# Feed-forward on one core: the first chunk's gate and up products by token tiles, its activations turned by four transposes

## The reference

```python
def swiglu(h, w_gate_up, w_down):
    g, u = jnp.split(h @ w_gate_up, 2, axis=-1)
    return (jax.nn.silu(g) * u) @ w_down
...
h = h + 0.5 * rmsnorm_2(swiglu_2(rmsnorm_2(h, gn[0]), ffn1_w_in[i], ffn1_w_out[i]), gn[1])
```

## Time and profile before

| what | value |
|---|---|
| median of 3 runs | 3369.08 us (3367.74 to 3376.34) |
| span of the profiled execution | 3369.5 us |
| PE busy (matmuls) | 2941.3 us, 87% |
| DVE busy | 1747.3 us, 52% |
| ACT busy | 1295.0 us, 38% |
| POOL busy | 226.9 us, 7% |
| HBM | 153 GB/s over the span |

### The profile page before, as it was taken

One profiled execution on the slowest core, in us unless ns is written; L12 is line 12 of the kernel. 1 busy time (PEld: TensorE's weight loads), 2 busy tenths in 40 slices (PEclk: granted clock), 3 DMA queues, 4 the chain that ended last, 5 costly groups with the idle time before them and its releaser, 6 DMA issues.

```text
span 3369.5 us, 48317 instructions
## 1 busy us (share of the span) xinstructions
PE 2941.3 (87%) x19034; PEld 2651.6 (79%) x19034; DVE 1747.3 (52%) x2004; ACT 1295.0 (38%) x1611; POOL 226.9 (7%) x300
## 2 busy tenths in 40 slices
PE   4977979779799887799899769989889899787799
PEld 4767967579799766699898659989779899775698
DVE  5556455564544544544545345454654544544544
ACT  3334333344333422343444344444443443422443
POOL 1110001110000111100000000000000000112000
PEclk9868988689899878899999779999899999878899
DMA  6445554555655420255454125555445555410353
GB/s 237 166 163 176 186 176 153 175 176 187 206 171 184 138 75 26 97 197 180 166 187 163 57 100 191 184 167 186 147 154 185 166 184 182 129 61 25 124 185 128
DMA packets 348861, 517.09 MB, mean 153 GB/s; under 512 B 9510, under 2 KB 303095, under 8 KB 341559
## 3 DMA queue, kind: packets, MB, share of 16 engines
q1 hardware_dynamic: 342320, 501.81, 44.8%
q0 software_dynamic: 3728, 10.34, 1.0%
q10 hardware_dynamic: 2678, 3.13, 0.3%
HBM read 513.40 MB, written 1.84 MB: 153 GB/s over the span
## 4 chain that ended last, share of the span: by engine, by line
PE 74%; DVE 11%; issue 5%; ACT 4%; DMA 2%; POOL 2%; ACTq 1%; DVEq 0%; POOLq 0%; SPq 0%
PE B L450 15%; PE B L451 15%; PE B L452 15%; PE Y L450 7%; PE Y L452 7%; PE Y L451 7%; DVE w_lo L1338 2%; DVE h_lo L1397 2%; PE Y L807 1%; ACT w_hi L956 1%; ACT junk L967 1%; DVE tmp L1366 1%; DVE x L1369 1%; DVE M L1460 1%; DMA raw<-in_w_ada 1%
## 5 line engine op out<-in xcount | busy, mean ns | idle before, releaser
L1338 DVE TENSOR_TENSOR w_lo<-raw,w_hi 128x2048 fp32r<-128x2048 f32 (+1 forms) x425 | 964.5, 2274 | 690.5 <-ACT w_hi L956 690.2
L450 PE MATMUL B<-h_hi,w_hi 128*128 128x256 f32 x4224 | 1215.3, 288 | 48.1 <-DVE h_lo L1397 19.6
L451 PE MATMUL B<-h_lo,w_hi 128*128 128x256 f32 x4224 | 1207.8, 286 | 0.0
L452 PE MATMUL B<-h_hi,w_lo 128*128 128x256 f32 x4224 | 1206.8, 286 | 0.0
L956 ACT ACTIVATE w_hi<-raw 128x2048 fp32r<-128x2048 f32 (+1 forms) x425 | 804.8, 1900 | 700.9 <-PE B L452 597.7
L450 PEld LDWEIGHTS B<-h_hi,w_hi 128*128 128x128 f32 x4224 | 819.4, 194 | 61.9 <-issue 51.4
L451 PEld LDWEIGHTS B<-h_lo,w_hi 128*128 128x128 f32 x4224 | 816.1, 193 | 5.7 <-issue 2.1
L452 PEld LDWEIGHTS B<-h_hi,w_lo 128*128 128x128 f32 x4224 | 817.1, 193 | 0.0
L450 PE MATMUL Y<-w_hi,a_hi 128*128 128x512 f32 (+1 forms) x810 | 318.1, 393 | 2.6 <-DVE w_lo L1338 2.6
L452 PE MATMUL Y<-w_hi,a_lo 128*128 128x512 f32 (+1 forms) x810 | 317.4, 392 | 0.0
L451 PE MATMUL Y<-w_lo,a_hi 128*128 128x512 f32 (+1 forms) x810 | 316.5, 391 | 0.0
(11 more groups left out here) (222 smaller groups left out, 2938.2 us busy)
## 6 DMA issues: line engine op xcount, KB each, us to landing
raw<-in_ffn_w_in SPq DMA_DIRECT2D x176, 1024.0 KB, 5.0
raw<-in_ffn_w_out SPq DMA_DIRECT2D x88, 1024.0 KB, 4.9
raw<-in_w_ada SPq DMA_DIRECT2D x56, 1024.0 KB, 5.0
raw<-in_w_gate_up SPq DMA_DIRECT2D x44, 1024.0 KB, 5.0
raw<-in_hgrn_w_in SPq DMA_DIRECT2D x32, 1024.0 KB, 5.4
raw<-in_w_down SPq DMA_DIRECT2D x22, 1024.0 KB, 5.0
raw<-in_w_in SPq DMA_DIRECT2D x14, 1024.0 KB, 5.7
raw<-in_diff_w_in SPq DMA_DIRECT2D x12, 1024.0 KB, 5.1
```

Source lines behind the costliest of these rows:

```text
L450: pe.matmul(o, lh, rh, start=first, stop=False)
L451: pe.matmul(o, lh, rl, start=False, stop=False)
L452: return pe.matmul(o, ll, rh, start=False, stop=last)
L1338: dve.tensor_tensor(w_lo[s][:, 0:n], raw[st.r % RING][:, 0:n], w_hi[s][:, 0:n].bitcast(F32), ALU.subtract).then_inc(unit_split, st.step("" ...
```

## The change

The first chunk's gate and up products are done by `first_pair` with `by_tokens`: a 128 by 128 piece of the input is the stationary operand, and 256 columns of the weights move. Each unit then has one half for each tile of tokens, of 8 x 3 = 24 matmuls. I call them gate-0 and gate-1, up-0 and up-1. PE's order is: transposes of tile 0, gate-0, transposes of tile 1, up-0, gate-1, up-1. The results have tokens on the partitions, so the product with silu in `tmp` must be turned for the down product: four transposes into the bank `B[2]`, placed behind the gate product of the second chunk, and `a_hi` and `a_lo` of the first chunk are read from `B[2]`.

```diff
--- before.py
+++ after.py
@@ -575,14 +575,17 @@
                     if t == 0:
                         pe.wait_ge(vector_step, st.at(f"{p}.{('loop', 'last')[i]}.act"))
 
-                whole_input(p)
-                stationary(B[0], f"{p}.first.gate", p)
-                stationary(B[1], f"{p}.first.up")
+                first_pair(p, ((by_tokens(B[0], CH), f"{p}.first.gate"), (by_tokens(B[1], CH), f"{p}.first.up")))
                 st.r += between and 1
                 pe.wait_ge(scalar_step, st.at(f"{p}.first.silu"))
                 stationary(B[0], f"{p}.second.gate")
+                pe.wait_ge(vector_step, st.at(f"{p}.first.mul"))
+                for c in range(2):
+                    for t in range(NT):
+                        mm = pe.transpose(B[2][:, c * S + t * P:c * S + t * P + P],
+                                          tmp[:, 2 * S + t * CH + c * P:2 * S + t * CH + c * P + P], ident[:, :])
+                mm.then_inc(tensor_step, st.step(f"{p}.first.turned"))
                 st.r += between and 1
-                pe.wait_ge(vector_step, st.at(f"{p}.first.mul"))
                 stationary(B[1], f"{p}.second.up")
                 st.r += between and 1
 
@@ -1014,7 +1017,9 @@
                     act.wait_ge(vector_step, st.at(f"{p}.{tag}.mul"))
                     if before:
                         act.wait_ge(unit_multiplied, st.at(f"{p}.{tag}.down"))
-                    act.activation(a_hi[:, 0:2, :].rearrange("p a b -> p (a b)"), tmp[:, 2 * S:4 * S], ACT.Copy)\
+                    else:
+                        act.wait_ge(tensor_step, st.at(f"{p}.{tag}.turned"))
+                    act.activation(a_hi[:, 0:2, :].rearrange("p a b -> p (a b)"), tmp[:, 2 * S:4 * S] if before else B[2], ACT.Copy)\
                         .then_inc(scalar_step, st.step(f"{p}.{tag}.ahi"))
 
                 body("first", None, False, skip)
@@ -1415,7 +1420,7 @@
                         between(1)
                     lo(KD * CH)
                     dve.wait_ge(scalar_step, st.at(f"{p}.{tag}.ahi"))
-                    tt(flat(a_lo[:, 0:2, :]), tmp[:, 2 * S:4 * S], flat(a_hi[:, 0:2, :].bitcast(F32)), ALU.subtract)\
+                    tt(flat(a_lo[:, 0:2, :]), tmp[:, 2 * S:4 * S] if before else B[2], flat(a_hi[:, 0:2, :].bitcast(F32)), ALU.subtract)\
                         .then_inc(vector_step, st.step(f"{p}.{tag}.act"))
 
                 body("first", None, False, 0)
```

## The result

The changed kernel takes 3405.62 us (median of 4 runs, 3401.94 to 3408.99) against 3369.07 us before: ratio 1.0096, 95% interval 1.0079 to 1.0114. It is slower by 36.5 us; forecast were 33 us and 3402 us, range 3384 to 3416. The profiled execution has a span of 3400.2 us, 30.7 us more than that of before. The interval of the ratio reaches from 27 to 38 us, so the two differences agree.

A forecast was written before the change was run, and what follows sets the result against it. PE, with 74% of the chain, was taken as the bound, waiting at boundaries for ACT, POOL and DVE. Terms: +30.1 us in seven plain feed-forwards, +7 in F, -4.1 in 0a, sum +33, 3402 us; range 3384 to 3416.

The forecast's parts named there:

- the seven plain stretches: Feed-forwards 0b, 1a, 1b, 2a, 2b, 3a, 3b, first transposes to first chunk's multiplication: pair ends 3.9 us later in each.
- F: Feed-forward with two passes, layers 0 and 1: +3.1 us each and 0.5 us each for `a_lo`, together +7 us.
- 0a: Feed-forward whose two weight units are split ahead of its boundary: pair ends 4.5 us earlier, -4.1 us with the transposes.
- Gate-0: First gate half, at 1a: starts at 1610.38, takes 5.0 us, ends at 1615.4.
- The shift: Tile 1's transposes, behind the first gate half, start 3.6 us later; the up weights (u0) come 3.3 us later.
- The second part: Up-0, gate-1 and up-1 after PE's idling: 8.4 us plus 2.2 for 4.4 us of low clock; pair ends 3.9 later.
- the signs: Expected in the changed profile: idle row before up-0 names DVE `w_lo` as releaser and is 5 to 7 us long.
- the clock pays it back: Rival: gate-0 and transposes wake the clock early and keep it up; +3 to +10 us, 3375 us, chance 0.09.
- The transposes: Four new transposes between two matmuls on PE, behind the second gate product: +0.4 us, bounds 0.3 and 0.8.
- The cover of d0: Before the down product: d0 usable 11.2 us after the pair's end, PE there at 11.6; cover 0.4 us, cost 0.
- d0 late: Rival: the chain to d0 takes 1 us more than its cover and all seven pay; 3409 us, chance 0.05.
- the gap pays: Rival: u0 ready when gate-0 ends, so all ten feed-forwards gain 4.1 us; -41 us, 3328 us, chance 0.05.

The follow-up runs named there:

- e3: Changed kernel with gate-1 ahead of up-0 in PE's order, u0's split left in place: 3377.35 us, ratio 1.0000.
- e6: Changed kernel with both tiles' transposes ahead of gate-0, then gate-0, up-0, gate-1, up-1: 3368.14 us, ratio 0.9980.
- e4: Changed kernel with both tiles' transposes first, then gate-0, gate-1, up-0, up-1, token form and turning kept: 3371.84 us, ratio 0.9997.
- e1: Changed kernel with u0 split earlier, behind tile 0's square sums on ACT and tile 0's residual on DVE: 3342.99 us, ratio 0.9911.
- e7: Changed kernel with u0 split between tile 0 and tile 1, ahead of tile 1's `h_hi` on ACT and `h_lo` on DVE: 3338.91 us, ratio 0.9896.
- e9: Changed kernel with 36 unused matmuls behind tile 1's transposes in the seven plain feed-forwards: 3409.48 us, ratio 1.0123.

## Why the prediction was right, step by step

By the profiles the change costs 30.7 us, and its terms make 30.8: 28.1 in the seven plain stretches, 4.1 in F, -4.9 in 0a, and 3.5 for the turning. Forecast were 33. The medians of the runs differ by 36.5 us; that the forecast lies between the two numbers is no proof of its terms, so here they are one by one. The 1.27 us with which the working begins go from this row of DVE at 1a in the kernel before to the first gate matmul (1615.40):

```profile
1614.13 2.16 DVE L1397 SCALAR_TENSOR_TENSOR h_lo<-Y,col,h_hi 128x128 fp32r<-128x128 f32 x8 [1.99 <-ACT h_hi L994]
```

1. **Gate-0.** It starts 4.68 us behind the first transposes, as worked out (1610.38 against 1605.71). From its start to that of the next work it takes 4.53 us at 1a (1613.84 to 1618.37) and 4.85 on average of the seven; forecast were 5.0.
2. **The shift.** Tile 1's transposes come 3.4 us later on average of the seven (9.53 us behind the first ones instead of 6.10; forecast 3.6), u0 2.95 us later (16.5 against 13.55; forecast 3.3). The eight take 1.03 to 1.19 us there instead of 1.97, since gate-0 had brought the clock back; for ACT's wait behind their start I had taken 0.9 us, a mean of high and low, and it was 0.64 (1618.37 to 1619.01).
3. **The second part.** The stretch of low clock from up-0 on is 5.2 us on average, not 4.4. The two misses, 0.4 us each, cancel, and that is luck: the pair ends 4.0 us later, forecast 3.9. Seven stretches give +28.1 us. PE waits 5.95 us for `w_lo` ahead of up-0, as the signs said (5 to 7 us), so the rival "the clock pays it back" did not occur: the granted clock fell in that gap. That the loss needs up-0 ahead of gate-1 is shown by e3, that it also needs gate-0 ahead of tile 1's transposes by e6.
4. **The transposes.** 1642.15 to 1642.50 is 0.35 us for four, and from the multiplication to the down product the plain ones take 11.53 us instead of 11.10, 0.43 us more. Forecast 0.4. The figure of the Trainium skill that I had set beside it (page "TensorE: Matmul & The Clock Gate", section "Part 4: PE-mode transpose", about 275 ns) is the duration of one here (L585, 0.27 us), not its price in a row of them; the trace decides for 0.09 us. The working beside it was wrong too: 0.7 us more in each of eight make 5.7 us, not some 7.
5. **The cover of d0.** It held: the down product has no wait in any of the seven, although `a_hi` starts 6.1 us behind the multiplication (1642.84 against 1636.73) and not 0.7 as before. By the rows of DVE d0 is usable at 1647.5 (1645.28 and half of 4.50), 0.8 us ahead of the down product (1648.30); worked out were 0.4. Its rival (d0 late) did not occur.
6. **F.** The mis-sized term. The stretches grew by 1.9 and 2.3 us, not by 3.1. The shift of the transposes was 1.8 and 1.9 us instead of 2.35, and the signal behind them came at the high clock. Nor does the later `a_lo` show a cost of 0.5 us: from the multiplication to the down product F takes 12.89 and 12.57 us, before 12.88 and 12.49. From there to the last chunk's multiplication both passes together take 1.0 us more, but in e4, with the same late `a_lo`, they take no more than before, so this is not shown to be its price.
7. **0a.** The pair ends 4.9 us earlier (forecast 4.5). With u0 in time e1 and e7 show the same for the others: 4.3 to 4.5 us in the plain ones and 6.0 to 6.3 us in F.

The rival "the gap pays" had the right price and the right condition. Its kernel is e7: 35 us faster than the kernel before, where 41 were worked out. In e7's profile the ten stretches are 47.1 us shorter than before. The rest is 14.8 us longer: 3.5 of these are the turning and some 8 the mixer stretch ahead of 3b, 472.3 us at a clock of 0.86 against 464.0 at 0.89.

## What to carry to other kernels

Before work is moved into an idle stretch of an engine, look at what that engine does for the others in it: eight transposes that had run 3.4 us earlier held u0 back, and u0 was not even a part of the moved work. A transfer or conversion that is hidden today has its place in a queue only because nobody waits for it; when the order of its readers changes, its own place must be looked at again. In this kernel two places on ACT and DVE made the difference between 1% slower and 1% faster, and the rows of the one boundary where u0 was ready already (0a) said ahead of any run that the new order gains there.

## What the runs showed of the hardware

- A POOL operation on 128 by 1 elements lasted 1.06 us instead of 0.19 while DVE subtracted two float32 tensors of 128 by 2048 in SBUF, and ended 0.05 us behind it (e1). In the kernel before, nine such operations overlap a low part on DVE: they take 1.3 to 2.1 us, and each ends 0.05 us behind one. Those that overlap nothing on DVE take 0.19 us, and so do eleven beside `h_lo`, which reads one of its two large inputs from `Y` in PSUM. In e1 this lengthened the chain of a boundary by 0.9 us; putting the DVE operation where POOL is not needed (e7) gave it back. The Trainium skill (page "GPSIMD Engine Reference", section "1. Specifications") says that GpSimd's SBUF interfaces are shared with VectorE, with contention when a DVE instruction has two SBUF inputs; the trace agrees, with 0.87 us for this pair.
- Filling matmuls of 4.56 us in a gap of 5.95 us kept the granted clock at 1.00, and the work behind took 2.5 us less in each of seven places (e9). The same program parts further on ran 13 us longer at a clock of 0.86 instead of 0.89. With equal mixers the rest of the program differed by up to 28 us between the profiles of the kernels. A few us saved by the clock at one place are not a few us of the whole time.
